# Group C's sample path on one Trainium2 core: rows ordered by sequence then head, four column tiles, values as the moving operand

## What is computed

```python
rel = relu(einsum('nqhe,nke->nqhk', iq, ik) * 64**-0.5)          # 8 index heads
score = einsum('nqhk,nqh->nqk', rel, iw * 8**-0.5)               # head sums
_, idx = top_k(where(visible, score, -inf), 129)                 # (512 + 4) // 4
logits = einsum('nqhd,nqkd->nhqk', q, k[idx]) * 128**-0.5
o = einsum('nhqk,nqkd->nqhd', softmax(logits), v[idx])
```

## Time and profile before

| quantity | value |
| --- | --- |
| median of 3 runs | 2926.79 us (2926.07 to 2928.79) |
| profiled execution, its time | 2930.68 us |
| its span in the trace | 2928.2 us |
| PE busy | 2746.4 us, 94% of the span |
| DVE, ACT, POOL busy | 1486.4, 916.8, 147.7 us |
| mean granted PE clock | 0.972 of 2.4 GHz |
| HBM traffic | 94 GB/s over the span |
| C's sample path in the first layer | 849.9 to 964.4 us of the span |

### The profile page before, as it was taken

One profiled execution on the slowest core, in us unless ns is written; L12 is line 12 of the kernel. 1 busy time (PEld: TensorE's weight loads), 2 busy tenths in 40 slices (PEclk: granted clock), 3 DMA queues, 4 the chain that ended last, 5 costly groups with the idle time before them and its releaser, 6 DMA issues. The chain is left out here.

```text
span 2928.2 us, 61465 instructions
## 1 busy us (share of the span) xinstructions
PE 2746.4 (94%) x25518; PEld 2533.6 (87%) x25518; DVE 1486.4 (51%) x2602; ACT 916.8 (31%) x1742; POOL 147.7 (5%) x301
## 2 busy tenths in 40 slices
PE   6999999999999988989989999999999999887998
PEld 6998988898787987889989899989878788787997
DVE  4333353236736586963343325432577268498433
ACT  3222342232222442232232224332333215323322
POOL 2100000000010000000001000100000200000001
PEclk8999999999999999989999999999999989998999
DMA  5323325632233222034333243265322422300543
GB/s 181 90 73 89 103 77 162 192 82 67 59 97 86 59 63 90 3 110 137 111 82 91 54 103 112 62 202 150 89 63 59 112 59 77 110 3 17 158 135 128
DMA packets 398475, 277.99 MB, mean 95 GB/s; under 512 B 34460, under 2 KB 368332, under 8 KB 394606
## 3 DMA queue, kind: packets, MB, share of 16 engines
q1 hardware_dynamic: 397278, 263.50, 32.5%
q10 hardware_dynamic: 912, 10.50, 0.9%
HBM read 237.75 MB, written 36.18 MB: 94 GB/s over the span
## 5 line engine op out<-in xcount | busy, mean ns | idle before, releaser
L326 PE MATMUL acc<-h_hi,in_w_hi 128*128 128x272 f32 x3968 | 888.1, 305 | 12.8 <-DVE in_w_lo L356 9.3
L326 PE MATMUL acc<-h_hi,in_w_lo 128*128 128x272 f32 x3968 | 824.2, 289 | 0.0
L326 PE MATMUL acc<-h_lo,in_w_hi 128*128 128x272 f32 x3968 | 822.7, 289 | 0.0
L326 PEld LDWEIGHTS acc<-h_hi,in_w_hi 128*128 128x128 f32 x3968 | 629.2, 190 | 97.5 <-issue 69.5
L326 PEld LDWEIGHTS acc<-h_lo,in_w_hi 128*128 128x128 f32 x3968 | 627.2, 190 | 0.0
L326 PEld LDWEIGHTS acc<-h_hi,in_w_lo 128*128 128x128 f32 x3968 | 624.2, 190 | 0.0
L356 DVE TENSOR_TENSOR in_w_lo<-in_w_raw,in_w_hi 128x512 fp32r<-128x512 f32 x496 | 345.9, 703 | 376.7 <-ACT in_w_hi L352 373.8
L352 ACT CAST in_w_hi<-in_w_raw 128x512 fp32r<-128x512 f32 x496 | 303.1, 617 | 367.8 <-PE acc L326 291.5
L326 PE MATMUL dr_bank<-over_both,out_weights 128*128 128x272 f32 x1984 | 280.2, 288 | 1.7 <-DVE over_both L713 1.7
L326 PEld LDWEIGHTS dr_bank<-over_both,out_weights 128*128 128x128 f32 x1984 | 260.7, 188 | 2.0 <-DVE over_both L713 2.0
L356 DVE TENSOR_TENSOR out_weights<-regions,out_weights 128x512 fp32r<-128x512 f32 x128 | 88.3, 692 | 184.1 <-ACT out_weights L352 184.0
(11 more groups left out here) (417 smaller groups left out, 3332.1 us busy)
## 6 DMA issues: line engine op xcount, KB each, us to landing
in_w_raw<-in_w_in SPq DMA_DIRECT2D x488, 256.0 KB, 2.9
region<-in_cache_sb_kv SPq DMA_DIRECT2D x128, 256.0 KB, 3.1
regions<-in_w_out SPq DMA_DIRECT2D x128, 256.0 KB, 2.8
regions<-in_cache_dsa SPq DMA_DIRECT2D x64, 160.0 KB, 2.2
region<-x_spill SPq DMA_DIRECT2D x32, 272.0 KB, 3.5
x_spill<-region SPq DMA_DIRECT2D x32, 272.0 KB, 2.1
mix_spill<-mix SPq DMA_DIRECT2D x6, 1088.0 KB, 5.4
mix_back<-mix_spill SPq DMA_DIRECT2D x6, 1088.0 KB, 7.4
```

The source lines that it names most:

```text
L326: last = pe.matmul(self.place(i)[:, c, 0:HALF_N], w[:, u % RING, t, :], part[f][:, HALF_N * c:HALF_N * c + HALF_N], start=first and w is k ...
```

## The change

- `related_at(s)` gives every sequence one of four 32-row places and one of two halves. The index products of four sequences go to four column tiles of one PSUM bank, and ACT rectifies four sequences at once (after s = 3 and s = 7).
- The head sums are taken once for eight sequences, after the rounds: 2 matmuls in place of 8. The same holds in the head.
- The 128 rows are ordered by sequence, then head. Logits take one 32-row tile for a pair of sequences. The index product and the logits of one round write different tiles.
- In the value step the probabilities (32 columns) are stationary and the values move (128 columns), in four tiles; odd and even sequences of a pair give two outputs, of which one half each is wanted. ACT copies both (`blocks`), PE turns them after one unit, and ACT copies the wanted parts to `mix`.
- Head weights come to the rows by two small matmuls with a 0/1 table (`token_of`), a mask and a sum on DVE, and a product on POOL; the transfers through HBM (9 DMAs) are gone. The table is 128x520 in place of 32x1024.

```diff
+def related_at(s):
+    place = (s + 1 + 2 * (s // 4)) % 4
+    return slice(NS * place, NS * place + NS), s // 4
...
         for s in range(NB):
-            last = pe.matmul(bank[0:NS, 0, NS * s:NS * s + NS], self.iq[:, s].rearrange("p r j t -> p (r j t)"), ft[:, 6, NP:NT], start=True, stop=True)
+            place, half = related_at(s)
+            last = pe.matmul(bank[place, 0, NS * half:NS * half + NS], self.iq[:, s].rearrange("p r j t -> p (r j t)"), ft[:, 6, NP:NT], start=True, stop=True)
         last.then_inc(self.related_n, 1)
+        for half in range(2):
+            pe.matmul(bank[:, 1, 64 + 8 * half:72 + 8 * half], self.token_of[:, half, :], tm[0:NS, QB, 320:328], start=True, stop=True)
...
-        for s in range(NB):
-            last = pe.matmul(bank[:, 0, 256:256 + NS], self.wx[:, s, :], self.rel_n[:, NS * s:NS * s + NS], start=(s == 0), stop=(s == NB - 1))
+        for half in range(2):
+            last = pe.matmul(bank[:, 0, 256:256 + NS], self.wx[:, half, :], self.rel_n[:, NS * half:NS * half + NS], start=(half == 0), stop=(half == 1))
...
-            if s >= 1:
-                pe.wait_ge(self.rectified_s, s)
...
                 if p == 0 and s >= 1:
+                    pe.wait_ge(self.copied_v, s)
                     pe.wait_ge(self.copied_s, s)
...
-            pe.matmul(bank[0:NS, 0, :], self.iq[:, s].rearrange("p r j t -> p (r j t)"), self.ikeys[:, s % 2, :], start=True, stop=True).then_inc(self.related, 1)
-            pe.matmul(bank[:, 3, :], self.qs[:, s].rearrange("p h c -> p (h c)"), self.keys[:, s % 2, :], start=(s == 0), stop=(s == NB - 1))
+            if s == 4:
+                pe.wait_ge(self.rectified_s, 1)
+            place, pair = related_at(s)[0], slice(NS * (s // 2), NS * (s // 2) + NS)
+            pe.matmul(bank[place, 2, :], self.iq[:, s].rearrange("p r j t -> p (r j t)"), self.ikeys[:, s % 2, :], start=True, stop=True).then_inc(self.related, 1)
+            pe.matmul(bank[pair, 3, :], self.qs[:, s, :], self.keys[:, s % 2, :], start=(s % 2 == 0), stop=(s % 2 == 1)).then_inc(self.scored, 1)
             yield 1
-            pe.wait_ge(self.rectified_s, s + 1)
-            pe.matmul(bank[:, 2, :], self.wx[:, s, :], self.rel_s[:, s % 2, :], start=(s == 0), stop=(s == NB - 1)).then_inc(self.scored, 1)
+        pe.wait_ge(self.rectified_s, 2)
+        for half in range(2):
+            last = pe.matmul(bank[:, 2, :], self.wx[:, half, :], self.rel_s[:, half, :], start=(half == 0), stop=(half == 1))
+        last.then_inc(self.scored, 1)
...
-        for s in range(NB):
+        for odd in range(2):
+            out = slice(P * odd, P * odd + P)
+            for j in range(4):
+                pe.matmul(bank[NS * j:NS * j + NS, 2, out], self.probT_s[0:NS, 4, NS * j:NS * j + NS], tm[0:NS, QB, P:2 * P], start=True, stop=False)
             for p in range(PAGES):
-                last = pe.matmul(mine(bank[:, 2, 0:P], s), ft[:, s, P * p:P * p + P], mine(self.probT_s[:, p, :], s), start=False, stop=(p == PAGES - 1), skip_group_check=True)
-            yield 0
+                for j in range(4):
+                    last = pe.matmul(bank[NS * j:NS * j + NS, 2, out], self.probT_s[:, p, NS * j:NS * j + NS], ft[:, 2 * j + odd, P * p:P * p + P],
+                                     start=False, stop=(p == PAGES - 1))
+        last.then_inc(self.applied_p, 1)
+        yield 1
+        pe.wait_ge(self.blocks_kept, 1)
+        for odd in range(2):
+            last = pe.transpose(bank[:, 3, P * odd:P * odd + P], self.blocks[:, P * odd:P * odd + P], k.c("ident"))
+        last.then_inc(self.blocks_turned, 1)
...
-        act.copy(k.mix[:, 0:4, NP:NT], bank[:, 2, 0:P].rearrange("p (h t) -> p h t", h=4)).then_inc(self.kept, 1)
+        act.copy(self.blocks, bank[:, 2, 0:2 * P]).then_inc(self.blocks_kept, 1)
+        act.wait_ge(self.blocks_turned, 1)
+        for odd in range(2):
+            act.copy(k.mix[:, 0:4, NP:NT].rearrange("p h (j x t) -> p x h j t", x=2, t=DS)[:, odd],
+                     bank[:, 3, P * odd:P * odd + P].rearrange("p (j x h t) -> p x h j t", x=2, h=4, t=DS)[:, odd]).then_inc(self.kept, 1)
...
+        step.then(dve.tensor_tensor(self.wv_heads, bank[:, 1, 64:80].rearrange("p (x h) -> p x h", x=2), self.head_of.unsqueeze(1).to_broadcast([P, 2, 8]), ALU.mult))
+        dve.tensor_reduce(self.wv, self.wv_heads, AX.X, ALU.add).then_inc(self.weights_made, 1)
...
-        pool.wait_ge(self.wv_loaded, 16 * 8)
-        pool.tensor_tensor(self.wx, self.wx, self.wv.unsqueeze(2).to_broadcast([NS, NB, P]), ALU.mult).then_inc(self.arranged, 1)
+        pool.wait_ge(self.weights_made, 1)
+        pool.tensor_tensor(self.wx, self.wx, self.wv.unsqueeze(2).to_broadcast([P, 2, P]), ALU.mult).then_inc(self.arranged, 1)
```

More of the change, by code:

```diff
@@ L119, in constants @@
     add("dsa_neg", np.where(i[None] <= i[:, None], 0, NEG))
-    row = np.arange(P) % NS
-    add("dsa_neg_s", np.where((row[:, None] // DS == t[None] // DS) & (t[None] <= row[:, None]), 0, NEG))
+    add("dsa_neg_s", np.where((i[:, None] // 16 == t[None] // DS) & (t[None] % DS <= i[:, None] % DS), 0, NEG))
     j, u = i[:, None] % C, np.arange(C)[None]
@@ L129, in constants @@
     add("chunk_in", np.broadcast_to(np.arange(NP) % C != 0, (P, NP)))
-    rt = np.arange(NS) % DS
-    add("spread", (rt[:, None, None] == row[None, None] % DS) & (np.arange(NB)[None, :, None] == row[None, None] // DS))
+    seq = np.zeros((P, 2), int)
+    for s in range(NB):
+        place, half = related_at(s)
+        seq[place, half] = s
+    add("spread", (seq[:, :, None] == i[None, None] // 16) & (i[:, None, None] % DS == i[None, None] % DS))
+    add("head_of", 2 * (i[:, None] // DS % 4) + i[:, None] // 16 % 2 == np.arange(8)[None])
+    add("token_of", t[:, None, None] == (DS * seq + i[:, None] % DS).T[None])
     return at, np.concatenate(parts, 1)
@@ L1744, in __init__ @@
         self.k, self.l, self.stream, self.bank, self.left = k, l, stream, bank, left
-        self.turned_in, self.rowed_v, self.rowed_s, self.weighed, self.stored, self.wv_stored, self.wv_loaded = (next(take) for _ in range(7))
+        self.turned_in, self.rowed_v, self.rowed_s, self.weighed, self.stored, self.weights_made = (next(take) for _ in range(6))
+        self.blocks_kept, self.blocks_turned = next(take), next(take)
         self.multiplied, self.rectified, self.added, self.looked, self.biased, self.exped, self.normed = (next(take) for _ in range(7))
@@ L1755, in __init__ @@
         self.iq = k.R1[:, 1640:1896].rearrange("p (s r j t) -> p s r j t", s=NB, r=2, j=4)
-        self.qs = k.R1[:, 1896:2920].rearrange("p (s h c) -> p s h c", s=NB, h=4)
-        self.wx = k.R1[0:NS, 2920:3944].rearrange("p (s c) -> p s c", s=NB)
+        self.qs = k.R1[:, 1896:2152].rearrange("p (s c) -> p s c", s=NB)
+        self.blocks = k.R1[:, 2152:2408]
+        self.choice = k.R1[:, 2920:3440]
+        self.wx = k.R1[:, 2920:3176].rearrange("p (x c) -> p x c", x=2)
+        self.head_of = k.R1[:, 3176:3184]
+        self.token_of = k.R1[0:NS, 3184:3440].rearrange("p (x c) -> p x c", x=2)
         self.work = k.R1[:, 2920:3432]
         self.qn = k.R1[:, 6280:6408]
-        self.wv = k.R1[0:NS, 3944:3952]
+        self.wv_heads = k.R1[:, 3440:3456].rearrange("p (x h) -> p x h", x=2)
+        self.wv = k.R1[:, 3944:3946]
         self.small = k.R1[:, 3952:3960].rearrange("p (x c) -> p x c", x=2)
@@ L1942, in act @@
         act.wait_ge(self.related_n, 1)
-        act.activation(self.rel_n, bank[0:NS, 0, 0:NB * NS], ACT.Relu, scale=0.125).then_inc(self.rectified_n, 1)
+        act.activation(self.rel_n, bank[:, 0, 0:2 * NS], ACT.Relu, scale=0.125).then_inc(self.rectified_n, 1)
         yield
@@ L1951, in act @@
             yield
-            act.wait_ge(self.related, s + 1)
-            if s >= 2:
-                act.wait_ge(self.scored, s - 1)
-            act.activation(self.rel_s[:, s % 2, :], bank[0:NS, 0, :], ACT.Relu, scale=0.125).then_inc(self.rectified_s, 1)
+            if s % 4 == 3:
+                act.wait_ge(self.related, s + 1)
+                act.activation(self.rel_s[:, s // 4, :], bank[:, 2, :], ACT.Relu, scale=0.125).then_inc(self.rectified_s, 1)
             yield
@@ L2047, in dve @@
             yield
-        dve.wait_ge(self.scored, NB)
+        dve.wait_ge(self.scored, NB + 1)
         dve.wait_ge(self.kept_n, 2)
@@ L2111, in sp @@
         store(k.s_dsa[bass.ds(l, 1)].rearrange("a n t w -> (a n t) w"), self.tm[0:NS, QB, 0:DSA_W])
-        sp.dma_start(k.sample_w, self.tm[0:NS, QB, 320:328]).then_inc(self.wv_stored, 16)
         yield 8
-        sp.wait_ge(self.wv_stored, 16)
-        load = Loads(sp, self.wv_loaded)
-        for r in range(2):
-            for j in range(4):
-                load(self.wv[16 * r + 4 * j:16 * r + 4 * j + 4, :], k.sample_w.rearrange("(s t) h -> h t s", t=DS)[2 * j + r])
         def load_page(g):
@@ L2131, in sp @@
         sp.wait_ge(self.biased, 13)
```

(2 more changed lines are left out.)

16 lines of the change are left out of this document (7 added, 9 removed).

## The result

The changed kernel takes 2890.06 us (median of 4 runs, 2885.08 to 2893.73), the kernel before 2927.79 us beside it: a ratio of 0.9863 (95% interval 0.9847 to 0.9878), or 37.7 us less. Forecast were 46.4 less.

The account below looks back on a forecast made before the run. PE, busy 94%, bounds the kernel; after the change SP's page supply bounds the rounds. Head -1.3, rounds -14.0 and value step -7.9 make -23.2 us per layer, -46.4 for two: 2926.8 becomes 2880.4 us, range 2869 to 2897.

Parts of the forecast that it names:

- Head: From L1848 to the first page transposes: fewer records on PE, 5.56 us to fall by 1.3 per layer.
- The chain of DVE and POOL: Head: small matmuls, two DVE operations and POOL's product, some 2 us, covered by three units of 2.25 us; nothing taken.
- Rounds: From the first page transposes through the head sums: 53.2 us to become 39.2, -14.0 per layer, bound by SP's page supply.
- PE's own part: Rounds without page waits: eight of 4.35 us plus the two head sums at the end, 37.0 us per layer.
- the supply's pace: Rounds: SP takes 1.10 us a page, 0.57 a weight load; last page ready 34.2 us in.
- the supply binds harder: Rounds: slow landings or waiting weight loads hold pages, 0.5 us more a round, 4 per layer: 2888.4 us; chance 0.13.
- Value step: Forty matmuls of 128 columns in groups of four tiles: 12.0 us to become 4.1, -7.9 per layer.
- After the meeting: Mixer D: transposes may gain 0.7 us, moved unit may lose 0.75 in the wait at L2227; nothing taken.
- Tiles that don't run together: Rounds, value step and head: matmuls in different tiles take turns, a round 5.41 us: 2907.4 us; chance 0.05.
- SP that does not bind: Rounds: page issue is faster or preloaded pages cover more, so PE's 37.0 us holds: 2876.0 us; chance 0.14.
- The clock at half through the rounds: PE's clock at half from the first page through the value step: +14.5 us per layer, 2955.8 us; chance 0.03.
- The rule of the Trainium skill: Tile groups cost 1.26 to 1.30 times one matmul: value step 0.85 us longer per layer, sum some 1.7 higher; not used.

Follow-up runs that it names:

- the page-number experiment: Changed kernel, but SP reads the numbers of pages 6 to 31 before the head and keeps them in registers; 2874.77 us, 0.9817 of the kernel before.
- the experiment above: Changed kernel with the value step alone in its old form (pages stationary, 16 probability columns moving, no unit in the tail); 2910.67 us, 0.9938 of the kernel before.

## Why the prediction was right, and where it was off

The sum was 8.7 us too large (46.4 against 37.7), and the measured time lies in the range. By the stage table, per layer and with means of the four stretches of each kernel:

- **Head**, forecast -1.3: 5.56 to 4.20, -1.36. The chain of DVE and POOL lies under the three units, as said. POOL's product took 0.61 us, the estimate was 0.65.
- **Rounds**, forecast -14.0 by a page supply that binds at 39.2: 53.16 to 41.86, -11.3. The mechanism was right, and the page-number experiment shows it. PE's own part came out at 36.8 without the supply, 37.0 forecast, by two errors that nearly cancel: a round takes 4.42 us and not 4.35, and the sums at the end take 1.3 up to the next unit and not 2.2. The term that was mis-sized is the supply's pace. In the first layer the last page went out (877.59 + 6.47 - 0.33) - 849.35 = 34.4 us after the first transposes, not 1.32 + 27.5 + 2.85 = 31.7. Of these 2.7 us, 1.95 are the 20 intervals between pages that follow each other: 18 take 1.16 to 1.18 us and two 1.48 and 1.50 (why is open), where 1.10 was read from six first issues, which test no slot. The earlier trace rows held the better row: two issues that test a slot in 1.51 us; with 0.33 for the last one, as a single page's issue lasts in the trace after, they are 1.18 apart. The first released page came 0.43 later, behind a weight load, and the five weight loads cost 0.33 more than priced. Landing and doubling of the last page took 0.3 more than said, and what follows it 0.65 less. This is worth 2.2 to 2.4 us in three of the stretches; the fourth, 42.92, is the one with the long issue of a weight load. The measured time lies nearer to the 2888.4 of the rival "the supply binds harder" than to the forecast. That rival was right by a steady price that it did not name; its own reasons, slow landings and weight loads that hold the pages, show in four of the twelve stretches of the experiments, in one of them of the changed kernel itself.
- **Choice**, forecast without change: 0.5 longer. Of this 0.3 is the mark, since the first stream row now starts beside the last head sum, 0.65 us ahead of the second one, where before it was 0.36.
- **Value step**, forecast -7.9 without the unit: 12.22 to 5.15 with it, -7.1, or -7.9 without its 0.87. The tile price was right (1.36 us for forty records, forecast 1.42); the first half ran at a clock of 0.60 and cost 0.7 more, and the end behind the records cost 0.4 less than said; that the total fits is in part luck.
- **After the meeting**, forecast without change beside the unit that leaves (-0.75): +0.4 on the mean of 128.09 to 129.65, so about 1.1 us per layer came back. Cut at mixer D's two long waits, the part reads nearly the same in all four stretches of each kernel. Up to the end of the wait at L2257, which stayed at 2.6 us, it is 2.1 shorter: the unit, and 1.4 more, as mixer D's first transposes and the units behind them did run at full clock. From there to the end of the wait at L2268 it is 2.2 longer (39.7 and 42.0). Of this 0.6 is that second wait, 2.7 us after the change; before it was

```profile
PE bank L2238 <- DVE regions L2360: 2.1, 1, 2.1
```

So the moved unit was mostly swallowed, as the prediction feared, but at a wait that its sum does not name. The other 1.6 is the clock, which fell behind the wait at L2257:

```profile
960.00:967.00 7.00, 5.97 (x32) 5.54 (x32) 6.96 (x15) 1.77 (x3) 0.00 (x0) 0.76 0.30 75
```

In the kernel before, the stretch behind the same wait is at full clock:

```profile
987.00:992.00 5.00, 4.80 (x35) 4.67 (x36) 3.46 (x10) 3.12 (x6) 0.00 (x0) 1.00 0.22 52
```

So the clock behind that wait is a cost that the sum did not have. With the page numbers ahead the same piece took 40.4 us, at a clock of 1.00 behind the same wait of 2.6; what decides between the two was not tried. Behind the second wait 0.3 is left. The stage varies from execution to execution, between 126.5 and 131.5 us over the variants with the same units or one more.

- The error of both layers follows: rounds 2.7, after the meeting 1.1, choice 0.5 are 4.3 per layer, 8.6 for two, of the 8.7 that the sum was off.
- **Rivals.** Tiles that don't run together: excluded, by 0.98 against 1.83 us for the pair and 1.36 against 4.6 in the value step. SP that does not bind: excluded, as the rounds fell by 5.0 us when it was relieved. The clock at half through the rounds: excluded; it read 1.00 there.
- **The rule of the Trainium skill** (page "TensorE: Matmul & The Clock Gate", section "Measured speedup vs the span model", 2.38 for three column tiles and 3.07 for four row tiles) was read by the prediction as a group that costs 1.26 to 1.30 times one matmul. Here a pair in two tiles cost 0.98 us against 0.95 for one, and four tiles of 128 columns gave 3.4, so a group of four cost 1.18 times one; the measurement decides. The 0.85 us that the prediction worked out by the rule are too many: they put the factor on 0.14 us, which was a group's price already.

## What to carry to other kernels

When PE's instructions between two waits are cut, price the queue that feeds them in the form that it has there: with its slot tests and with what stands between two issues, not the unhindered burst at the start. If a dynamic transfer costs as much queue time for reading its address as for issuing, read the addresses while the queue is idle; here that brought 16.3 us, nearly half as much as the change itself, 10.1 of it in the rounds. And compare stages, not spans: the first two spans differed by 7.6 us more than the change had brought, by chance in the forecast's favour.

## What the runs showed of the hardware

- Two 512-column matmuls of 32 output rows take 0.98 us up to the unit behind them in two column tiles and 1.83 in one; a single one takes 0.95.
- A page load by a number read from memory holds SP for 1.16 to 1.18 us in 18 of 20 cases; with the number in a register two follow each other in 0.91 - 0.33 = 0.58.
- PE's granted clock stood at 0.50 behind the 3.9 us wait at L1909 (the first row), and at 1.00 in the same place when units shortened that wait to 1.0 us (the second):

```profile
931.00:935.00 4.00, 3.53 (x16) 3.46 (x17) 1.89 (x4) 0.00 (x0) 0.00 (x0) 0.50 0.27 66
```

```profile
925.00:935.00 10.00, 8.87 (x127) 7.46 (x125) 4.61 (x10) 3.22 (x8) 0.00 (x0) 1.00 0.34 80
```

- Once down, it stayed at 0.50 for all of the 16 us of old value matmuls in the experiment above, and came back within 6 us in the changed kernel's value step. What tells the two apart was not tried.
